# Seven products of sums for eight in 18 of the 22 gate-and-up pairs of each feed-forward

## What is computed

```python
SEQ, D_MODEL, D_FF = 512, 1024, 2816        # D_FF_2 is 2816 as well

def swiglu(x, w_gate, w_up, w_down):
    return (jax.nn.silu(x @ w_gate) * (x @ w_up)) @ w_down

# first block
h = h + 0.5 * swiglu(rmsnorm(h, ffn1_norm), ffn1_w_gate, ffn1_w_up, ffn1_w_down)
...   # three attentions (forgetting, selected keys, memory), gated and summed
h = h + 0.5 * swiglu(rmsnorm(h, ffn2_norm), ffn2_w_gate, ffn2_w_up, ffn2_w_down)
# second block
...   # a causal convolution over 31 tokens and trailing means over 2 to 16
h = h + swiglu_2(rmsnorm_2(h, g_ffn), w_gate, w_up, w_down)
return rmsnorm_2(h, g_final)
```

## Time and profile before

| | |
|---|---|
| median of three runs | 1778.28 us (1775.78 to 1778.55) |
| profiled execution: span | 1773.8 us (its own time is not printed) |
| PE busy | 1762.3 us (99%) |
| PEld busy | 1433.6 us (81%) |
| DVE busy | 690.0 us (39%) |
| ACT busy | 699.3 us (39%) |
| POOL busy | 805.8 us (45%) |

### The profile page before, as it was taken

One profiled execution on the slowest core, in us unless ns is written; L12 is line 12 of the kernel. 1 busy time (PEld: TensorE's weight loads), 2 busy tenths in 40 slices (PEclk: granted clock), 3 DMA queues, 4 the chain that ended last, 5 costly groups with the idle time before them and its releaser, 6 DMA issues.

```text
span 1773.8 us, 23396 instructions
## 1 busy us (share of the span) xinstructions
PE 1762.3 (99%) x8496; PEld 1433.6 (81%) x8496; DVE 690.0 (39%) x1137; ACT 699.3 (39%) x1124; POOL 805.8 (45%) x373
## 2 busy tenths in 40 slices
PE   9999999999999999999999999999999999999998
PEld 7888888888888777788888888888867888888887
DVE  5222240068867885236352222200775522222002
ACT  5232231166554477785242322221425432222212
POOL 2444445457665433324554444444533444444443
PEclk9999999999999999999999999999999999999999
DMA  5222222332333121112222222222351222222222
GB/s 175 102 99 95 95 95 95 112 107 90 104 119 110 67 76 38 49 48 95 96 95 95 98 101 96 95 95 95 101 143 64 91 99 101 96 95 95 95 96 82
DMA packets 50494, 168.22 MB, mean 95 GB/s; under 512 B 6264, under 2 KB 7032, under 8 KB 50304
## 3 DMA queue, kind: packets, MB, share of 16 engines
q1 hardware_dynamic: 47088, 161.34, 26.7%
q10 hardware_dynamic: 3344, 6.05, 1.2%
HBM read 161.84 MB, written 2.11 MB: 92 GB/s over the span
## 4 chain that ended last, share of the span: by engine, by line
PE 96%; issue 1%; DVE 1%; POOL 1%; ACT 1%; DMA 0%; POOLq 0%; SPq 0%; ACTq 0%; DVEq 0%
PE bank L533 27%; PE bank L534 27%; PE bank L535 27%; PE bank L753 8%; PE bank L798 2%; PE bank L824 2%; PE bank L926 1%; PE bank L815 1%; POOL weights_low L444 1%; PE bank L612 0%; PE bank L666 0%; DMA residual<-x_t 0%; PE bank L604 0%; PE bank L667 0%; DVE bank L1589 0%
## 5 line engine op out<-in xcount | busy, mean ns | idle before, releaser
L444 POOL TENSOR_TENSOR weights_low<-raw_weights,weights_high 128x1024 fp32r<-128x1024 f32 x292 | 706.0, 2421 | 874.2 <-ACT weights_high L1043 846.2
L533 PE MATMUL bank<-input_high,weights_high 128*128 128x512 f32 x1424 | 557.3, 391 | 1.8 <-DVE input_low L1434 1.0
L534 PE MATMUL bank<-input_high,weights_low 128*128 128x512 f32 x1424 | 554.3, 389 | 0.0
L535 PE MATMUL bank<-input_low,weights_high 128*128 128x512 f32 x1424 | 554.3, 389 | 0.0
L1043 ACT CAST weights_high<-raw_weights 128x1024 fp32r<-128x1024 f32 x294 | 306.3, 1044 | 306.8 <-DMA raw_weights<-weights 288.3
L533 PEld LDWEIGHTS bank<-input_high,weights_high 128*128 128x128 f32 x1424 | 267.3, 188 | 61.5 <-issue 4.3
L535 PEld LDWEIGHTS bank<-input_low,weights_high 128*128 128x128 f32 x1424 | 267.3, 188 | 55.8
L534 PEld LDWEIGHTS bank<-input_high,weights_low 128*128 128x128 f32 x1424 | 267.4, 188 | 54.6 <-issue 0.2
L533 PE MATMUL bank<-hidden_high,weights_high 128*128 (+1 forms) x528 | 205.4, 389 | 0.0
L534 PE MATMUL bank<-hidden_high,weights_low 128*128 (+1 forms) x528 | 205.4, 389 | 0.0
L535 PE MATMUL bank<-hidden_low,weights_high 128*128 (+1 forms) x528 | 205.4, 389 | 0.0
(11 more groups left out here) (258 smaller groups left out, 1845.4 us busy)
## 6 DMA issues: line engine op xcount, KB each, us to landing
raw_weights<-weights SPq DMA_DIRECT2D x294, 512.0 KB, 3.4
out_t<-out_t SPq DMA_DIRECT2D x8, 256.0 KB, 2.3
residual<-x_t SPq DMA_DIRECT2D x6, 256.0 KB, 5.7
glu_stacked<-glu_padded ACTq DMA_DIRECT2D x24, 64.0 KB, 3.9
glu_stacked<-glu_padded SPq DMA_DIRECT2D x24, 64.0 KB, 3.6
mem_in<-mem_t ACTq DMA_DIRECT2D x1, 1024.0 KB, 4.9
tile<-forget_sums ACTq DMA_DIRECT2D x4, 256.0 KB, 3.5
raw_weights<-weights SPq DMA_DIRECT2D x3, 256.0 KB, 5.6
```

Of the source, the lines that this page charges most:

```text
L444: pool.tensor_tensor(wl[:, u % RING, :], raw[:, u % RING, :], wh[:, u % RING, :].bitcast(F32), ALU.subtract).then_inc(low_done, 1)
L533: pe.matmul(out, wh[:, u % RING, w], rh, start=start, stop=False)
L534: pe.matmul(out, wl[:, u % RING, w], rh, start=False, stop=False)
L535: return pe.matmul(out, wh[:, u % RING, w], rl, start=False, stop=stop)
```

## The change

In each of the three feed-forwards the first four pairs in the new order stay as they were ("plain": hidden channels 18 to 21 of 22, so that the unit order changes on the host), and the other 18 become "mixed". For a mixed pair the two weight units and the 8 input chunks are seen as a 2 x 2 of blocks: gate and up by the first and the second four chunks; and the tokens fall in two halves of 256. Strassen's scheme then takes seven products of 4 chunks x 3 matmuls x 256 columns, 84 matmuls, where there were 48 of 512 columns. Called by their input block, in TensorE's order, the products are G, E, B22, D, F, B11 and B21.

What this needs:

- *Mixed inputs*, once for each stage: for each k of 4, seven blocks of 128 x 256 (`xmix`). VectorE makes a set of eight (`mixed_input`: two scaled copies of `h`, which take the factor `rstd` in, one subtraction of 512 and two operations of 256), ACT casts the high parts of seven (1792 elements), the low parts are subtracted by POOL for k = 0, 1 and by VectorE for k = 2, 3. Sets use two buffers, so set k waits for the low part of set k-2. These steps stand between the plain pairs on each engine.
- *Weight sums*, for each mixed pair: VectorE makes three sums of 128 x 512 and one in place of the gate weights (`weight_sums`), ACT casts three of 512 more, POOL takes the low parts of the first two sums and VectorE that of the third. The high parts of the two units are cast behind them, since the gate unit itself is changed, and POOL's low parts of the units stand behind its low parts of the sums.
- *Combining*: ACT copies the sixth product out of PSUM (`take_sixth`), VectorE puts the products together (`combine`: six operations of 256 to 512 elements for each row, one input of each of them in PSUM) and multiplies gate by up. The factor is in the inputs by then, so the two scalings of a pair go.
- *The hidden values* are stored as float32 in the gate-and-up stage. They are split in the down stage: ACT casts and VectorE subtracts 22 times there (`hidden_split`, `split_hidden`), the first four splits inside the last two pairs.

The diff, cut to its core:

```diff
+PLAIN = 4
+MIXED = FC - PLAIN
+HALF = S // 2
...
+            def mixed_input_low(name, k):
+                pool.wait_ge(sem("xmix_high"), before(name, 4) + k + 1)
+                pool.tensor_tensor(xmix[k][:, :, HALF:], xsum[k % 2][:, 0:7, :], xmix[k][:, :, 0:HALF].bitcast(F32),
+                                   ALU.subtract).then_inc(sem("xmix_low_first"), 1)
+
+            def gate_up_lows(name, first, u0):
+                for u in range(first, u0 + 2 * PLAIN):
+                    low_part(u)
+                    if u in (u0 + 4, u0 + 5):
+                        mixed_input_low(name, u - u0 - 4)
+                with pool.Fori(0, MIXED // 2) as i:
+                    for c in range(2):
+                        u = u0 + 2 * (PLAIN + c)
+                        for e in range(2):
+                            pool.wait_ge(sem("sum_high"), before(name, 54) + i * 6 + (3 * c + e + 1))
...
+                            pool.tensor_tensor(sum_l[e][:, :], sums[e][:, :], sum_h[e][:, :].bitcast(F32), ALU.subtract
+                                               ).then_inc(sem("sum_low"), 1)
+                        pool.wait_ge(high_done, i * 4 + (u + 2))
+                        for s in (u % RING, (u + 1) % RING):
+                            pool.tensor_tensor(wl[:, s, :], raw[:, s, :], wh[:, s, :].bitcast(F32), ALU.subtract
+                                               ).then_inc(low_done, 1)
...
+            def mixed_product(out, high, low, of):
+                for k in range(4):
+                    w = slice(k * P, (k + 1) * P)
+                    pe.matmul(out, high[:, w], xmix[k][:, of, 0:HALF], start=k == 0, stop=False)
+                    pe.matmul(out, low[:, w], xmix[k][:, of, 0:HALF], start=False, stop=False)
+                    mm = pe.matmul(out, high[:, w], xmix[k][:, of, HALF:], start=False, stop=k == 3)
+                return mm
+
+            def mixed_pair(name, i, c, u):
...
+                pe.wait_ge(sem("sum_low"), before(name, 36) + i * 4 + (2 * c + 1))
+                mixed_product(bank[b + 1][:, first], sum_h[0], sum_l[0], G_OF).then_inc(sem("sums_read"), 1)
+                pe.wait_ge(sem("sum_low"), before(name, 36) + i * 4 + (2 * c + 2))
+                mixed_product(bank[b][:, second], sum_h[1], sum_l[1], E_OF).then_inc(sem("sums_read"), 1)
+                pe.wait_ge(sem("last_sum_low"), before(name, 18) + i * 2 + (c + 1))
+                mixed_product(bank[b + 2][:, second], sum_h[2], sum_l[2], B22).then_inc(sem("sums_read"), 1)
+                pe.wait_ge(low_done, i * 4 + (u + 1))
+                mixed_product(bank[b + 1][:, second], wh[:, gate, 0:S], wl[:, gate, 0:S], D_OF)
+                mixed_product(bank[b + 2][:, first], wh[:, gate, S:2 * S], wl[:, gate, S:2 * S], F_OF).then_inc(unit_done, 1)
+                pe.wait_ge(low_done, i * 4 + (u + 2))
+                mixed_product(bank[b][:, first], wh[:, up, 0:S], wl[:, up, 0:S], B11).then_inc(sem("six"), 1)
+                mixed_product(bank[b + 3][:, first], wh[:, up, S:2 * S], wl[:, up, S:2 * S], B21).then_inc(unit_done, 1)
...
+            def sum_highs(q, i=None):
...
+                act.copy(sum_h[0][:, :], sums[0][:, :]).then_inc(sem("sum_high"), 1)
+                high(u + 1, i=i)
...
+                act.copy(sum_h[1][:, :], sums[1][:, :]).then_inc(sem("sum_high"), 1)
...
+                high(u, i=i)
...
+                act.copy(sum_h[2][:, :], sums[2][:, :]).then_inc(sem("sum_high"), 1)
+
+                for c in range(PLAIN):
+                    if c == 2 or (u0 and c < 2):
+                        after(u0 + 2 * c)
...
+                    silu(c % 2, c + 1)
+                    if c == 2 or (u0 and c == 1):
+                        after(u0 + 2 * c + 1)
+                    if c == 0:
+                        mixed_input(0)
+                        mixed_input(1)
+                    elif c < 3:
+                        mixed_input(c + 1)
+                    if c == 2:
+                        sum_highs(0)
+                sum_highs(1)
+                with act.Fori(0, MIXED // 2 - 1) as i:
+                    for c in range(2):
+                        take_sixth(c, i * 2 + (c + 1))
+                        silu(c, i * 2 + (PLAIN + c + 1))
+                        sum_highs(c + 2, i)
...
+                def weight_sums(q, i=None):
...
+                    dve.tensor_tensor(sums[0][:, :], gate[:, 0:S], gate[:, S:2 * S], ALU.add).then_inc(sem("sums"), 1)
...
+                    dve.tensor_tensor(sums[1][:, :], sums[0][:, :], up[:, 0:S], ALU.add).then_inc(sem("sums"), 1)
+                    dve.tensor_tensor(gate[:, 0:S], gate[:, 0:S], up[:, 0:S], ALU.add).then_inc(sem("sums"), 1)
...
+                    dve.tensor_tensor(sums[2][:, :], sums[1][:, :], up[:, S:2 * S], ALU.add).then_inc(sem("sums"), 1)
+                    dve.wait_ge(sem("sum_high"), before(name, 54) + at(3 * q + 3, 6))
+                    dve.tensor_tensor(sum_l[2][:, :], sums[2][:, :], sum_h[2][:, :].bitcast(F32), ALU.subtract
+                                      ).then_inc(sem("last_sum_low"), 1)
...
+                plain(0)
+                mixed_input(0)
+                mixed_input(1)
+                plain(1)
+                mixed_input(2)
+                mixed_input_low(2)
+                mixed_input(3)
+                plain(2)
+                mixed_input_low(3)
+                weight_sums(0)
+                plain(3)
+                weight_sums(1)
+                for first, end, t in ((0, 6, hid_a), (6, MIXED // 2 - 1, hid_b)):
+                    with dve.Fori(first, end) as i:
+                        for c in range(2):
+                            f = bass.ds(i * 2 + (c - 2 * first), 1)
+                            combine(c, t[:, f, :].rearrange("p a (b n) -> p (a b) n", n=HALF), i)
+                            weight_sums(c + 2, i)
+                combine(MIXED - 2, halves_of(hidden(MIXED - 2)))
+                split_hidden(name, 0, 4)
+                combine(MIXED - 1, halves_of(hidden(MIXED - 1)))
...
+            def hidden_split(name, f):
+                act.wait_ge(sem("ff_hidden"), before(name, FC) + (PLAIN + f + 1 if f < MIXED else f - MIXED + 1))
+                act.copy(hidden_high(f), hidden(f)).then_inc(sem("ff_high"), 1)
```

More of the change, by code:

```diff
@@ L1189, in rotary_tables, with down @@
                                ).then_inc(sem("sine"), 1)
-            def down(u0, loads=(), between=None):
-                for f in range(2):
+            def down(name, u0, loads=(), between=None):
+                for f in range(FC - 2):
                     after(u0 + f)
-                if between:
-                    between()
-                with act.Fori(0, (FC - 6) // 4) as i:
-                    for c in range(4):
-                        after(u0 + 2 + c, i)
-                for f in range(FC - 4, FC - 2):
-                    after(u0 + f)
+                    if f == 0:
+                        act.wait_ge(unit_done, u0)
+                    for j in ((2 * f + 4, 2 * f + 5) if f < 2 else (f + 6,) if f + 6 < FC else ()):
+                        hidden_split(name, j)
+                    if f == 1 and between:
+                        between()
                 for dst, src, name in loads:
@@ L1518, in stepped, with split_hidden @@
+            def split_hidden(name, first, end):
+                for f in range(first, end):
+                    dve.wait_ge(sem("ff_high"), before(name, FC) + f + 1)
+                    dve.tensor_tensor(hidden_low(f), hidden(f), hidden_high(f).bitcast(F32), ALU.subtract
+                                      ).then_inc(sem("ff_split"), 1)
             def stepped():
@@ L1915, in gate_up_units @@
 def gate_up_units(gate, up):
-    g, u = column_units(gate), column_units(up)
+    order = [*range(MIXED, FC), *range(MIXED)]
+    g, u = column_units(gate)[order], column_units(up)[order]
     return np.stack([g, u], axis=1).reshape(-1, P, DK * P)
```

236 lines of the change are left out of this document (163 added, 73 removed).

## The result

The changed kernel takes 1825.43 us, the median of four runs (1824.11 to 1825.82), beside 1778.01 us before (1775.78 to 1778.55): a ratio of 1.0269, 95% interval 1.0254 to 1.0283. It is 47.4 us slower, where 1828.6 was forecast. The profiled execution took 1825.82 us with a span of 1824.0; the span of before was 1773.8, so the spans lie 50.2 us apart.

What follows compares the result with a forecast made beforehand. TensorE bounds the kernel before; the port shared by VectorE and POOL sets the mixed pairs. Starts 51.2 plus down stages 8.7 less pairs 9.6 give +50.3; 1773.8+50.3+4.5 = 1828.6 us, range 1795 to 1865.

Steps and rivals of the forecast that it cites:

- a mixed pair: Steady gate-and-up work: falls from TensorE's 10.88 us to 10.75, set by the port VectorE and POOL share, not to 10.04.
- 18 mixed pairs of a stage: Gate and up: first pair 10.04 us, second about 10.55, sixteen at 10.75; 192.6 against 195.8, 3.2 gained a stage.
- starts of the three stages: Plain pairs: making mixed inputs on the in-order queues delays casts and low parts; 19.0, 16.1, 16.1 us late, together 51.2.
- down stages: Down parts: first splits and casts delay TensorE 2.4 us a stage, rotary tables 1.5 more in the first; together 8.7.
- what lies around the span: Whole run: the median of 1778.3 lies 4.5 us above the profiled span of 1773.8, added to the forecast.
- The port's exclusion: VectorE operations with both inputs in SBUF and POOL's take turns, whole operation by operation; each VectorE one costs POOL 0.46 us.
- the signs that the prediction named: Mixed pairs: weight sums above 1 us, low sums above 1.3, wait some 0.7; plain pairs: TensorE idle 5 to 10.
- The clock rival: Stage starts: TensorE's clock falls after stalls above 5 us, costing 7.2 us a stage, 21.6 in all, 1850; chance 0.15.
- the wait for the last pair's banks: Start of each down stage: four first splits ahead of the last combining free the banks late; 1.7 us.
- the second unit's: Start of each down stage: the second down unit's cast stands behind the last pair's SiLU; 0.7 us late.
- the stall behind the rotary tables: First down stage: tables stand behind four more splits and hold ACT's weight casts; 7.4 us, all but 1.5 covered.
- The rival with TensorE as the bound: Mixed pairs: TensorE, not the port, sets the pair; 34 us less than forecast, 1795; chance 0.12.

Runs made afterwards that it cites:

- sum-lows kernel: Changed kernel with the low parts of a pair's first two weight sums subtracted by VectorE instead of POOL; 1791.45 us, ratio 1.0081.
- the kernel with the added matmuls: Changed kernel with TensorE running matmuls into an unused bank where it stood still in the plain pairs; 1825.12 us, ratio 1.0271.
- four-plain-pairs kernel: Changed kernel plus sum low parts on VectorE, two first splits behind the last combining, and reordered stage starts, still four plain pairs; 1762.9 us.
- six-plain-pairs kernel: Changed kernel plus sum low parts on VectorE, two first splits behind the last combining, and reordered starts with six plain pairs; 1741.21 us.

## Why the prediction held

| step | forecast | measured |
|---|---|---|
| a mixed pair | 10.75 us, set by the port | 10.73; 10.08 with 1.3 us less on the port |
| 18 mixed pairs of a stage | 192.6 | 192.1, 192.6, 192.5 |
| starts of the three stages | 19.0, 16.1, 16.1 late | 18.6, 15.6, 15.7 |
| down stages | 3.9, 2.4, 2.4 longer | 3.8, 2.3, 2.3 |
| growth of the span | 50.3 | 50.2 |
| what lies around the span | 4.5 | 1.8 |

**The port's exclusion** (rows 6 and 7) was the step that decided. The sum-lows kernel confirms it by its sign: more work on VectorE, shorter pairs. The hand-overs are in the rows of the mixed pair: from 1066.17 POOL's 1.24 and VectorE's 0.55 fill 1.79 with nothing between, and POOL woke 0.08 behind VectorE, where 0.15 was the estimate. So the engines meet not at semaphores alone, as the part ahead of the prediction has it, but also at this port. Of the signs that the prediction named, POOL's low sums average 1.48 us, and TensorE waits 0.65 a pair, most of it ahead of the second product (0.50 between starts for 0.12). VectorE's weight sums are the weak one: only the last is stretched much, to 1.79, and the mean of the four is 1.00, no more than the bound that was set.

**The starts** came out right in their sum and partly wrong inside. Stalls of 5.2, 1.4, 7.3 and 2.2 were forecast ahead of units 4 to 7; the trace has 4.9, 0, 5.7 and 0 in the second stage, and slow matmuls in units 4 and 6 instead. The clock rival, which I gave 0.15, was right on the event (the granted clock fell in each of the three stages) and wrong on its price. I had charged it 7.2 us a stage, what a whole unit at half speed costs less what the next low part covers. At the low level TensorE lost less than that: unit 4 took 2.9 us longer than its 5.4 and unit 6 2.1, some 5 us in the second stage before anything covers it, where two times 5.4 was assumed. And units 5 and 7 had those low parts to wait for anyway, as the kernel with the added matmuls shows. The Trainium skill, TensorE: Matmul & The Clock Gate, section "HAM oscillation — how this bites in real kernels", has each wait between bursts pay anew for the clock; the falls agree with it (0.77 on the first matmul behind the wait), the payment doesn't in this kernel (47.9 us behind before with the clock kept up in units 4 to 6, 47.4 without), and does in the four-plain-pairs kernel (1.6 us a fall).

**The down stage**: the wait for the last pair's banks, forecast as 1.7, is 1.4; the second unit's, forecast as 0.7, is 0.6; the stall behind the rotary tables, 1.5, is 1.4.

**What was luck.** The 50.3 and 50.2 agree better than their parts. The stages grew by 48.0: the starts and the down stages cost 1.6 us less than forecast and the mixed pairs gave 0.7 more. The other 2.2 lie outside the three feed-forwards, for which the forecast had nothing; 1.5 of it is the end of the run, which takes from 13.2 to 14.8 us in the kernels of this record.

**What was mis-sized** is small. The span of before belonged to an execution near the lowest of its runs (1775.78), with some 2 us around it, and I took the distance from the median, 4.5; this made the forecast 1828.6 in place of 1825.9. TensorE's pace for a mixed pair is 10.08 and not 10.04: 84 x 0.12, where 21 starts had given 0.1195. The rival with TensorE as the bound (1795) is what the sum-lows kernel turned into, 1791.5.

## What to carry to other kernels

A scheme that trades matmuls for element-wise work must be priced on the engines that do that work, and where VectorE and POOL shut each other out their times add: here 0.8 us saved on TensorE in a pair was worth 0.15, until two operations went from POOL to VectorE, which does them in half the time. One-off work put between the first units of a pipeline belongs behind the casts and low parts of the next units, on every in-order queue, with enough plain work ahead to cover it; taking one stall away alone only moves it to the next. An earlier start for a helper can cost more than it gives, if it lets loose an operation that holds what the path needs.

## What the runs showed of the hardware that was not expected

After the stalls of some 5 us TensorE's clock was at its lower level, 1.2 GHz of 2.4: matmuls of 512 columns took 0.77 on the first row behind the wait in place of 0.39. A stall of 3.7 us between starts in the four-plain-pairs kernel was followed by a fall in the second stage and by none in the third, and one of 2.2 us likewise by a fall there and by none in the six-plain-pairs kernel: the length of the stall alone doesn't tell whether the clock falls.
